# Sampled tokens' outer products as one fp32r matmul with three stacked terms, with the HGRN norm and the projections in another order

## The reference

```
# HGRN2, per sequence b and each of 8 heads (keys 128, values 128)
s_new = exp(g_last)[..., None] * s + einsum('bhsd,bhsv->bhdv', ki * exp(g_last - G), vi)
# mLSTM, per sequence b and each of 4 heads (keys 256, values 256)
C_new = decay * C + einsum('bhs,bhsd,bhsv->bhdv', w_state, ki, vi)
```

## Time and profile before

| | |
|---|---|
| median of 3 runs | 2771.38 us (2754.73 to 2779.73) |
| profiled execution, span from the first to the last instruction | 2776.0 us |
| TensorE, VectorE, ScalarE, GpSimd busy | 93%, 46%, 32%, 10% of the span |
| HBM read, written | 439.10 MB, 29.92 MB |

### The profile page before, as it was taken

The page is one execution under the profiler, slowest core; times in us unless marked ns, Lnnn a source line. Parts: engine busy times, 40 slices in busy tenths (PEclk is TensorE's granted clock), DMA queues, the critical chain, the costliest instruction groups (busy, mean ns, idle before and its releaser), DMA issues.

```text
span 2776.0 us, 27585 instructions
## 1 busy us (share of the span) xinstructions
PE 2589.6 (93%) x10948; PEld 1888.2 (68%) x10948; DVE 1289.5 (46%) x1610; ACT 900.8 (32%) x1039; POOL 278.0 (10%) x271
## 2 busy tenths in 40 slices
PE   8999989999899999999989999899979989998996
PEld 5666666666577665765766666677767767776774
DVE  2544346221100011453345321277867858776784
ACT  3231121010111003231121010266646646655663
POOL 1321203000000001230203000000000000000000
PEclk9999989999999999999679999899999999999998
DMA  5212334433144552123323533289969969996991
GB/s 177 91 65 91 95 104 148 159 121 122 31 121 121 132 157 86 67 95 91 95 70 125 186 106 108 91 289 319 339 205 321 334 223 325 313 316 226 320 335 63
DMA packets 392203, 470.71 MB, mean 170 GB/s; under 512 B 14218, under 2 KB 315546, under 8 KB 392088
## 3 DMA queue, kind: packets, MB, share of 16 engines
q1 hardware_dynamic: 368060, 376.76, 42.5%
q0 software_dynamic: 23936, 92.28, 8.8%
q10 hardware_dynamic: 92, 0.00, 0.0%
HBM read 439.10 MB, written 29.92 MB: 169 GB/s over the span
## 4 chain that ended last, share of the span: by engine, by line
PE 78%; DVE 9%; ACT 5%; issue 4%; DMA 2%; SPq 0%; POOL 0%; DVEq 0%; ACTq 0%; POOLq 0%
PE bank L421 25%; PE bank L435 6%; PE bank L708 5%; DVE w_rest L1431 5%; PE bank L710 5%; PE bank L709 5%; PE bank L918 4%; PE bank L933 3%; PE bank L923 3%; PE bank L459 2%; ACT w_high L1050 2%; PE bank L656 2%; PE bank L721 2%; PE bank L665 2%; PE bank L522 1%
## 5 line engine op out<-in xcount | busy, mean ns | idle before, releaser
L421 PE MATMUL bank<-arena,weights 128*128 128x320 f32 x2560 | 712.0, 438 | 13.4 <-ACT arena L1029 7.6
L421 PEld LDWEIGHTS bank<-arena,weights 128*128 128x128 f32 x2560 | 489.7, 193 | 217.8 <-issue 8.2
L1431 DVE TENSOR_TENSOR w_rest<-weights,w_high 128x2048 fp32r<-128x2048 f32 x176 | 395.0, 2286 | 17.1 <-ACT w_high L1044 16.8
L1044 ACT ACTIVATE w_high<-weights 128x2048 fp32r<-128x2048 f32 x176 | 326.4, 1904 | 5.5 <-DMA weights<-in_w_ex_up 5.4
L708 PE MATMUL bank<-w_high,tokens_high 128*128 128x512 f32 x704 | 285.2, 405 | 30.4 <-DVE w_rest L1431 21.4
L710 PE MATMUL bank<-w_high,tokens_rest 128*128 128x512 f32 x704 | 278.9, 396 | 0.0
L709 PE MATMUL bank<-w_rest,tokens_high 128*128 128x512 f32 x704 | 277.2, 394 | 0.0
L1437 DVE TENSOR_TENSOR w_rest<-weights,w_high 128x2048 fp32r<-128x2048 f32 x88 | 201.6, 2292 | 127.2 <-ACT w_high L1050 126.7
L1050 ACT ACTIVATE w_high<-weights 128x2048 fp32r<-128x2048 f32 x88 | 168.6, 1916 | 186.0 <-PE bank L710 160.6
L708 PEld LDWEIGHTS bank<-w_high,tokens_high 128*128 128x128 f32 x704 | 132.9, 189 | 79.0 <-DVE w_rest L1431 41.1
L435 PE MATMUL bank<-weights,arena 128*128 128x512 f32 (+1 forms) x384 | 167.4, 593 | 0.0
(11 more groups left out here) (341 smaller groups left out, 3140.6 us busy)
## 6 DMA issues: line engine op xcount, KB each, us to landing
weights<-in_w_ex_gate SPq DMA_DIRECT2D x88, 1024.0 KB, 6.0
weights<-in_w_ex_up SPq DMA_DIRECT2D x88, 1024.0 KB, 8.6
weights<-in_w_ex_down POOLq DMA_DIRECT2D x88, 1024.0 KB, 7.0
weights<-in_w_in SPq DMA_DIRECT2D x36, 2048.0 KB, 7.7
weights<-in_state_mlstm_c SPq DMA_DIRECT2D x8, 2048.0 KB, 8.2
out_c_sample<-weights SPq DMA_DIRECT2D x8, 2048.0 KB, 7.5
weights<-in_w_ff_gate SPq DMA_DIRECT2D x22, 512.0 KB, 3.9
weights<-in_w_ff_up SPq DMA_DIRECT2D x22, 512.0 KB, 5.1
```

Source lines behind the costliest of these rows:

```text
L421: mm = nc.tensor.matmul(out[:, 0:T], w[:, k, chunk(m)], src[:, k, :], start=k == 0, stop=k == KC - 1)
L1044: nc.scalar.activation(w1h[s][:, k], mo_w1[s][:, k], ACT.Copy).then_inc(mo_w1h[s], 1)
L1431: ins = nc.vector.tensor_tensor(w1l[s][:, k], mo_w1[s][:, k], w1h[s][:, k], ALU.subtract)
```

## The change

1. Three terms in one matmul. For each half `g` of the sampled tokens (32 tokens, 4 sequences) the keys and values are split into a rounded part and a difference, and stacked in rows: keys high, rest, high (rows in the order that fits `g`) and values high, high, rest. One fp32r matmul over 96 rows then sums the three terms. ScalarE writes the rounded copies (32 rows by 1024 columns, or by 256 per mLSTM head), VectorE the differences, into `kstA`, `vstA`, `kstB`, `vstB`. The rows for padding, and the memsets that zeroed them, go.
2. GpSimd masks 96 stacked rows with one of four columns (`seg4`) into fp32r buffers `km`, used for both mixers; it waits for the differences ("parts A", "parts B").
3. The HGRN norms of all 8 heads move behind the last mLSTM update and the scaling of `hB` on VectorE.
4. The projections are ordered `ga`, `bo`, `gb`, `pa`, `pb`, `wo`, with the head sums `muB` after `ga` and `varB` after `bo`; the ring's strips are in the same order. `sigmoid(ga)` is kept whole in `gaS`, and VectorE multiplies `pa` by it straight out of PSUM, after `hBo`.

```
-    for name in ("pa", "ga", "bo", "gb", "pb", "wo"):
+    for name in ("ga", "bo", "gb", "pa", "pb", "wo"):
...
-        kmA = [view(a_x1 + i * D, D) for i in range(2)]
+        km = [rounded(f"keys_of_one{i}", a_x1 + i * D, D) for i in range(2)]
+        kstA, vstA = [[rounded(f"{n}_parts_hgrn{g}", aligned(a_x) + (2 * i + g) * D, D) for g in range(2)]
+                      for i, n in enumerate(("keys", "values"))]
...
-                            mm = nc.tensor.matmul(out[:, chunk(j)], kmA[b % 2][:, chunk(h)], vTok[:, 2, chunk(h)],
+                            mm = nc.tensor.matmul(out[:, chunk(j)], km[b % 2][0:96, chunk(h)], vstA[b // 4][0:96, chunk(h)],
...
-                            mm = nc.tensor.matmul(out[:, c * 256:(c + 1) * 256], kmB[b % 2][:, kc],
-                                                  vB[:, 2, h * 256:(h + 1) * 256], start=True, stop=True)
+                            mm = nc.tensor.matmul(out[:, c * 256:(c + 1) * 256], km[b % 2][0:96, kc],
+                                                  vstB[b // 4][0:96, h * 256:(h + 1) * 256], start=True, stop=True)
...
+                project_all("ga", xT)
+                head_sums(l, "muB", hB, HB, 2, dv_s, "hB", l)
+                project_all("bo", xT)
+                head_sums(l, "varB", sqB, HB, 2, ac_s, "sqB", l)
+                project_all("gb", xT)
                 pe.wait_ge(*dv_s.at("oA", l))
                 project_all("pa", oA)
-                head_sums(l, "muB", hB, HB, 2, dv_s, "hB", l)
-                project_all("ga", xT)
-                head_sums(l, "varB", sqB, HB, 2, ac_s, "sqB", l)
-                project_all("bo", xT)
-                project_all("gb", xT)
...
+                    if hf == 1:
+                        act.wait_ge(*dv_s.at("qS", l, 1))
...
+                        for g in range(2):
+                            r = slice(32 * g, 32 * g + 32)
+                            step()
+                            nc.scalar.activation(kstA[g][r], kTok[r, 2, :], ACT.Copy).then_inc(*ac_s.done())
+                            nc.scalar.activation(kstA[g][64:96], kTok[r, 2, :], ACT.Copy).then_inc(*ac_s.done("keys A", l, g))
+                            step()
+                            nc.scalar.activation(vstA[g][r], vTok[r, 2, :], ACT.Copy).then_inc(*ac_s.done())
+                            nc.scalar.activation(vstA[g][32 - 32 * g:64 - 32 * g], vTok[r, 2, :], ACT.Copy)\
+                                .then_inc(*ac_s.done("values A", l, g))
...
+                    if h == HB - 1:
+                        act.wait_ge(*pe_s.at("ktB", l, h, 2))
...
+                            nc.scalar.activation(vstB[g][r], vB[r, 2, :], ACT.Copy).then_inc(*ac_s.done())
...
+                    act.wait_ge(*dv_s.at("ktB", l, h, 2))
+                    for g in range(2):
+                        r, n = slice(32 * g, 32 * g + 32), slice(256 * h, 256 * h + 256)
+                        nc.scalar.activation(kstB[g][r, n], kTB[r, 2, n], ACT.Copy).then_inc(*ac_s.done())
+                        nc.scalar.activation(kstB[g][64:96, n], kTB[r, 2, n], ACT.Copy).then_inc(*ac_s.done("keys B", l, h, g))
...
-                        nc.vector.memset(kTok[NS:P, 2, :], 0.0).then_inc(*dv_s.done())
-                        nc.vector.memset(vTok[NS:P, 2, :], 0.0).then_inc(*dv_s.done("rows padded", l))
...
+                for g in range(2):
+                    r, other = slice(32 * g, 32 * g + 32), slice(32 - 32 * g, 64 - 32 * g)
+                    dve.wait_ge(*ac_s.at("keys A", l, g))
+                    nc.vector.tensor_tensor(kstA[g][other], kTok[r, 2, :], kstA[g][r], ALU.subtract).then_inc(*dv_s.done())
+                    dve.wait_ge(*ac_s.at("values A", l, g))
+                    nc.vector.tensor_tensor(vstA[g][64:96], vTok[r, 2, :], vstA[g][r], ALU.subtract)\
+                        .then_inc(*dv_s.done("parts A", l))
...
-                nc.vector.memset(kTB[NS:P, 2, :], 0.0).then_inc(*dv_s.done("keys padded", l))
...
-                    if b == 0:
-                        dve.wait_ge(*ac_s.at("rsA", l))
-                        dve.wait_ge(*ac_s.at("silu g", l))
-                    hgrn_norm(b)
...
+                dve.wait_ge(*ac_s.at("rsA", l))
+                dve.wait_ge(*ac_s.at("silu g", l))
+                for h in range(HA):
+                    hgrn_norm(h)
...
+                dve.wait_ge(*ac_s.at("ga", l))
+                for m in range(KC):
+                    dve.wait_ge(*pe_s.at("mm", l, "pa", m // 4, m % 4))
+                    nc.vector.tensor_tensor(yA[:, m, :], of(l, "pa", m // 4, m % 4)[:, 0:T], gaS[:, m, :], ALU.mult)\
+                        .then_inc(*free(dv_s, l, "pa", m // 4, m % 4))
...
-                    nc.gpsimd.tensor_scalar(kmA[b % 2], kTok[:, 2, :], seg[:, b:b + 1], None, ALU.mult)\
+                    nc.gpsimd.tensor_scalar(km[b % 2][0:96], kstA[b // 4][0:96], seg4[0:96, b % 4:b % 4 + 1], None, ALU.mult)\
...
-                    nc.gpsimd.tensor_scalar(kmB[b % 2], kTB[:, 2, :], seg[:, b:b + 1], None, ALU.mult)\
+                    nc.gpsimd.tensor_scalar(km[b % 2][0:96], kstB[b // 4][0:96], seg4[0:96, b % 4:b % 4 + 1], None, ALU.mult)\
```

More of the change, by code:

```diff
@@ L135, in rounded, with aligned @@
             return v
+        def aligned(a):
+            return -(-a // 8) * 8
         def place(n):
@@ L170, in build @@
         seg = view(place(DB), DB)
+        seg4 = view(place(4), 4)
         blk4 = view(place(32), 32)
@@ L235, in build @@
         sW = [view(a_att + 896 + i * 448, 448) for i in range(2)]
-        kmB = [view(a_x1 + i * D, D) for i in range(2)]
+        vstB, kstB = [[rounded(f"{n}_parts_mlstm{g}", aligned(a_x) + (2 + 2 * i) * H + g * D, D) for g in range(2)]
+                      for i, n in enumerate(("values", "keys"))]
         cvg = view(a_v, KC, 27)
@@ L244, in build @@
         nrowP = view(a_v + 2688, P, rows=8)
-        tg = [view(a_att + i * T, T) for i in range(2)]
         decB = view(place(HB * DB), HB, DB)
@@ L253, in build @@
         gbS = view(a_x + 4 * H, KC, T)
+        gaS = view(a_u, KC, T)
         yA = view(a_g, KC, T)
@@ L332, in build @@
         row2 = view(a_g + 5 * P + 1, 1, dt=I32)
+        row34 = view(a_g + 5 * P + 2, 1, dt=I32)
         laterT = view(a_g + 6 * P, P)
@@ L505, in sampled_hgrn @@
                 pe.wait_ge(*dv_s.at("qS", l, 1))
-                pe.wait_ge(*dv_s.at("rows padded", l))
+                pe.wait_ge(*dv_s.at("parts A", l))
                 for b in range(DB):
@@ L1178, in _ @@
                     table[("act", "st", l, hf)] = ac_s.count
+                    if hf == 1:
+                        act.wait_ge(*dv_s.at("qS", l, 1))
+                        act.wait_ge(*ac_s.at("v", l, "v", 1, 2))
+                        act.wait_ge(*ac_s.at("kt", l, 1, 2))
+                        for g in range(2):
[7 more added lines that the diff above has]
+                                .then_inc(*ac_s.done("values A", l, g))
                     while todo:
@@ L1258, in _, with gate_tiles @@
                 table[("act", "nro", l)] = ac_s.count
[L1260 to L1276, removed]
+                def gate_tiles(name, dst):
                     for i in range(2):
@@ L1282, in _ @@
                     table[("act", name, l)] = ac_s.count
+                gate_tiles("ga", gaS)
+                act.wait_ge(*dv_s.at("xcB", l, HB - 1))
+                nc.scalar.activation(sqB, hB, ACT.Square).then_inc(*ac_s.done("sqB", l))
+                gate_tiles("bo", boS)
+                act.wait_ge(*dv_s.at("oA", l))
+                for h in range(HB):
+                    act.wait_ge(*pe_s.at("varB", l, h))
+                    nc.scalar.activation(rsB[:, h, :], of(l, "varB", h)[:, 0:T], ACT.Sqrt, bias=eps, scale=1.0 / 256)\
+                        .then_inc(*free(ac_s, l, "varB", h))
+                table[("act", "rsB", l)] = ac_s.count
+                gate_tiles("gb", gbS)
                 norm(l, "1", x1T, x1T)
@@ L1321, in _ @@
             settle()
+            nc.vector.tensor_scalar(row34, row3, 3, None, ALU.bitwise_and).then_inc(*dv_s.done())
+            settle()
+            nc.vector.tensor_tensor(seg4, colI[:, 0:4], row34.broadcast_to([P, 4]), ALU.is_equal).then_inc(*dv_s.done())
             nc.vector.tensor_copy(xorF, xorI).then_inc(*dv_s.done())
@@ L1750, in _ @@
                     table[("dve", "nS", l, h)] = dv_s.count
+                    for g in range(2):
+                        r, other = slice(32 * g, 32 * g + 32), slice(32 - 32 * g, 64 - 32 * g)
+                        n = slice(256 * h, 256 * h + 256)
+                        dve.wait_ge(*ac_s.at("keys B", l, h, g))
+                        nc.vector.tensor_tensor(kstB[g][other, n], kTB[r, 2, n], kstB[g][r, n], ALU.subtract)\
+                            .then_inc(*dv_s.done())
+                        if h == HB - 1:
+                            nc.vector.tensor_tensor(vstB[g][64:96], vB[r, 2, :], vstB[g][r], ALU.subtract)\
```

(14 more changed lines are left out.)

11 lines of the change are left out of this document (5 added, 6 removed).

## The result

The changed kernel takes 2736.35 us (median of 12 runs, 2733.45 to 2740.58); the kernel before, run beside it, takes 2754.16 (12 runs, 2749.53 to 2779.73). The medians differ by 17.8 us, a ratio of 0.9935; the ratio estimated over all runs is 0.9924, 95% interval 0.9901 to 0.9947. The interval leaves out 1, though single runs of before differ by up to 30 us.

What follows compares the result with a forecast made beforehand. TensorE, busy for 93% of the span, was taken as the bound. Terms 23.5 + 3.5 + 5 + 1.8 = 34 us off 2776.0; the same share off the median 2771.38 gives 2738, rounded to 2740, range 2716 to 2768.

Steps and rivals of the forecast that it cites:

- The mLSTM outer products: mLSTM update: one fp32r record per matmul cuts the outer products from 3.97 to 2.5 us a round, saving 23.5 us.
- Putting the norms behind the updates is part of the gain: mLSTM update, VectorE: updates plus a norm take 6.5 us, over the 6.1 us round; moved norms hide under `ga`.
- `oA`, 3.5 us: Projections after the mLSTM update: `pa`'s 1.75 us wait for the last norm goes in either layer, saving 3.5 us.
- The memset, 1.8 us: Between the last HGRN update and the block weights: removing a padding memset saves 0.9 us a layer, 1.8 us.
- Copies and differences: ScalarE's rounded copies and VectorE's differences, ahead of HGRN and in the mLSTM heads, put nothing on the path.
- HGRN's round and its clock: HGRN update: 24 records instead of 32, rounds of 5.1 us, at 1.2 GHz in both layers.
- The net of it: HGRN update: layer 1 saves 12 us from 44.7, layer 0 loses 7 from 25.5; net 5 us saved.
- Keeps its 4 us stall ahead and streams at most half of what it does now: HGRN update: reason given for 1.2 GHz in both layers, since layer 1 stayed there with more streaming.
- (1): Rival: the mLSTM update falls to 1.2 GHz from small idles, rounds of 10.1 us, 2802 us; chance 0.08.
- (2): Rival: HGRN keeps 2.4 GHz in both layers, saving 26 and 7 us, 2709 us; chance 0.12.
- (3): Rival: outer products don't get cheaper, fp32r at 256 columns costing as fp32 does, 2762 us; chance 0.08.
- (4): Rival: GpSimd takes twice as long for fp32r keys, making both rounds 6.3 us, 2757 us; chance 0.08.

Runs made afterwards that it cites:

- Experiment 3: The changed kernel with one HGRN head's norm back behind each mLSTM round's updates; 2736.3 us, ratio 0.9943.
- the earlier trace: The profile of the kernel before from which the prediction was read; span 2776.0 us, with HGRN at 1.2 GHz in layer 1.
- the usual one: A second profile of the unedited kernel before, with HGRN rounds of 3.57 us in layer 1; 2754.0 us, span 2752.4.
- experiment 6: The changed kernel with HGRN's outer products in fp32 over 128 rows, half of them zeros, mLSTM still fp32r; 2724.03 us, ratio 0.9877.
- Experiments 1: The changed kernel with HGRN's outer products back in fp32 over 64 rows, mLSTM still fp32r; 2763.75 us, ratio 1.0043.
- experiment 5: The kernel before with HGRN's outer products reading only the 64 rows that hold data, not the 64 zero rows; 2797.95 us, ratio 1.0146.
- experiment 2: The changed kernel with ten unused fp32r matmuls of 512 columns added to each HGRN round; 2792.26 us, ratio 1.0152.
- Experiment 9: The changed kernel, HGRN in fp32r, with the gate projections and SyncE's store of the prompt's HGRN state issued earlier; 2734.18 us, ratio 0.9901.
- h1: The kernel of experiment 6 with the gate projections and SyncE's store of the prompt's HGRN state issued earlier; 2707.49 us, ratio 0.9821.

## Why the prediction was right, and which steps of it were not

2740 was forecast and 2736 measured, inside the range. Most of its terms held. One baseline did not, and its error had the size of the gain.

- **The mLSTM outer products: right.** Forecast: a round of 6.1 us, idle before the third and the fourth head, released by VectorE's update, 23.5 us in all. Measured 6.1, 0.67 and 0.15 us there, and 2 x 11.7 = 23.4. The price was near: in the group of four the second record starts 0.23 us after the first, the third and the fourth 0.12 and 0.11 after the one ahead. From the first pair to the next read it is 451.76 - 449.26 = 2.50 us, as forecast, though the fourth pair starts at 2.07 and not at 2.2, and the read follows it after 0.43.
- **"Putting the norms behind the updates is part of the gain": wrong.** Experiment 3 has them in the rounds, at the same time. I had added 4 x 0.80 + 3.26 = 6.5; the updates come at 0.69, so 2.75 + 3.19 + 0.17 = 6.1 fits. The cover I named for them held all the same. VectorE after the update of layer 0, in the changed kernel:

```profile
491.26 2.15 DVE L1788 RECIPROCAL arena<-arena 128x320 f32<-128x320 f32 x1
...
516.29 0.49 DVE L1793 TENSOR_TENSOR arena<-arena 128x320 f32<-128x320 f32 x1
527.92 0.82 DVE L1818 SCALAR_TENSOR_TENSOR arena<-bank,arena 128x640 f32<-128x640 f32 x1 [11.14 <-PE bank L538]
```

  The norms end at 516.8, and VectorE then waits 11.14 us for TensorE; the forecast had 8.
- **`oA`, 3.5 us: right**, in the projections' idle time above. **The memset, 1.8 us: too small.** TensorE's idle ahead of the block weights was 2.00 us in layer 0 of the execution of the earlier trace rows and 1.68 in the usual one; it is 0.36 now, some 3 us over two layers. The term had left out, for one, the 0.28 us for which VectorE stood idle ahead of the memset. **Copies and differences: right.** From the end of the HGRN update to the start of the mLSTM update TensorE takes 81.7 us in either layer, 83.5 and 84.0 in the usual execution, so they put nothing on its path.
- **HGRN's round and its clock: right. The net of it: wrong.** Both layers run at 0.50 with 24 records and 5.12 us a round, as forecast (5.1). But "layer 1 now" was costed from the earlier trace rows, and most executions of before are not like that. Against these the split loses in both layers, 7.7 + 7.2 = 15 us, where I wrote 5 saved; experiment 6 (2724 us), without the split in HGRN, confirms the sign and 12 of the 15. The error and its remedy were in the text: the same stall, 4.18 and 4.12 us, had led to two clocks in one execution, and three runs of before differed by 25 us. I took the state of one layer in one execution as that kernel's property.
- **Why the total was still close.** Forecast 34 us off 2776.0, i.e. 2742; found 16.4 off 2752.4. The 20 us that I had wrongly counted as gained in HGRN are, but for 1, the 19 by which layer 1 of the profiled execution lay above the usual one. The end was right because forecast and measurement both have HGRN at 1.2 GHz in both layers; the difference to before was twice too large. That the clock came out as forecast was in part luck, since the reason given for it does not hold as it stands (next point).
- **"Keeps its 4 us stall ahead and streams at most half of what it does now", hence 1.2 GHz: the forecast held, the reason only in part.** The clock is lost before the stall. TensorE in layer 0 of the changed kernel, and the table by stretch there:

```profile
311.98 2.00 PE L509 MATMUL bank<-arena 64*128 64x64 f32 x16
313.90 1.95 PE L519 MATMUL bank<-arena,weights 128*128 128x8 f32 x16
316.00:318.00 2.00, 2.00 (x12) 2.00 (x10) 1.97 (x2) 0.71 (x1) 0.43 (x1) 0.50 0.00 0
```

  It is 0.50 at 316 to 318 us, with TensorE busy throughout, behind 16 records of 64 columns and 16 of 8; the stall of 4.34 us begins at 320.8. Both profiles of before have 0.50 there too; in that of the earlier trace rows it is back at 1.00 ahead of the stall (320 to 322 us), at 0.50 behind it (324 to 328), and at 1.00 from 330 on. Experiments 1 and 5 ran at 1.2 GHz with as many records and as many columns as before, and only fewer rows; experiment 2 streamed far more and stayed there. Experiment 9 rules out the stall as what holds the fp32r rounds. What I had not thought of is that half of the rows were zeros and still counted. Whether the fp32r rounds fail for their 96 rows, their 24 records or fp32r itself was not separated: no run had fp32r over 128 rows, or fp32 over 96.
- **The rivals.** (1) The clock of the mLSTM update was 1.00, with 0.67 and 0.15 us of idle in a round: it did not fall. The Trainium skill's case that I cited (TensorE: Matmul & The Clock Gate, "A second HAM failure mode: psum-queue depth-cycling"), a clock that swings under small idles between groups, was not borne out here. (2) HGRN at 2.4 GHz needs other records: h1 has it, with fp32 over 128 rows. (3) fp32r at 256 columns was cheaper. (4) GpSimd's keys cost the same in fp32r, in a group of the changed kernel to compare with the 2847 ns of the earlier trace rows:

```profile
L1945 POOL TENSOR_SCALAR keys_of_one<-keys_parts_mlstm,arena x16: 2839/2842/2846, 439.4 to 1493.5; 96x1024 fp32r<-96x1024 f32 x16
```

  The load of 128 fp32r weights, 188 ns in the mLSTM update (fp32: 193), shows no fast path, as weighed there.
- **Transfers.** The store of a C strip now takes 10.5 us at the median, 7.5 in the earlier trace rows, and a load 8.2, 8.8 there; no wait of TensorE in this stage ends with a transfer, so the 7 us of cover held.

What stays open: why a round over 64 rows takes 7.22 us at 1.2 GHz, and one over 128 rows 6.83; what a 128-column fp32r record costs at 2.4 GHz, which no run reached; and what, in before, decides in a run whether layer 1 gets its clock back after the stall.

## What to carry to other kernels

Before a stage's present cost is a term of a sum, see whether it is the same in every layer and in several executions: two layers of one program at different granted clocks, or a spread between runs of the size of the gain, say that the baseline itself is one of the unknowns. An edit that removes zero rows from a stretch that is paced by weight loads may cost its clock (experiment 5), and so did here one that put fp32r records over 96 rows in place of twice as many over 128; so weigh it by stage and keep the part that gains: fp32r in the mLSTM update, fp32 over 128 rows in HGRN. A stall is followed through all the queues that its release passes, since an earlier chain on VectorE gained nothing until SyncE's store was also moved (2756 and 2707 us).

## What the hardware showed that I had not expected

- Zero rows counted. The same HGRN records over 64 rows instead of 128, half of them zeros, ran at 0.50 in both layers, where the usual execution has 1.00, and the kernel before took 2798 us instead of 2753 (experiment 5).
- At clock 0.50, a TensorE that was busy for 50 of 50 us with 512-column records among the others stayed at 0.50 (experiment 2).
- With the same records over 128 rows, a stall of 4.2 us was followed in layer 1 by a clock of 0.50 in one execution and of 1.00 in another (the earlier trace rows and the usual execution); without a stall the clock was 1.00 from the second round on, in both layers (experiment 8).
